# A state-space scan made in one pass from masked decay matrices, among the projections, in place of seven halving rounds

## The reference, cut to what matters

```python
def ssd_scan(x, dt, a, bm, cm, d_skip, s0):      # Q = 128
    cum = jnp.cumsum(dtc * a.astype(F32), axis=2)
    xdt = xc * dtc[..., None]
    diff = cum[:, :, :, None] - cum[:, :, None, :]
    seg = masked_decay(diff, causal)               # one number per (i, j, head)
    scores = jnp.einsum('bcihn,bcjhn->bcijh', cc, bc) * seg
    y_intra = jnp.einsum('bcijh,bcjhp->bcihp', scores, xdt)
    # chunk states, carried over the chunks, then y_inter, then + x * d_skip
```

## Time and profile before

| | us |
|---|---|
| three runs | 3509.2, 3509.12, 3503.52 (median 3509.12) |
| the profiled execution, and its span | 3511.4, 3509.3 |
| TensorE busy, share of the span | 3158.2, 90% |
| VectorE, ScalarE, GpSimd busy | 1349.5, 970.1, 243.9 |
| mean granted TensorE clock, share of full speed | 0.934 |

### The profile page before, as it was taken

How to read it: one execution, slowest core, us unless ns; L and a number is a source line. 1 busy time by engine, 2 the same in 40 slices (tenths; PEclk the granted TensorE clock), 3 DMA queues, 4 the chain that set the end, 5 groups by cost and what they waited for, 6 DMA issues and landing times. The chain is left out here.

```text
span 3509.3 us, 48131 instructions
## 1 busy us (share of the span) xinstructions
PE 3158.2 (90%) x20921; PEld 2703.4 (77%) x20921; DVE 1349.5 (38%) x1691; ACT 970.1 (28%) x1326; POOL 243.9 (7%) x136
## 2 busy tenths in 40 slices
PE   6999997778889979999979999986898898899996
PEld 5999994456546669999969999844555474899996
DVE  3233234562734252322352323355436342523235
ACT  3222213232334242222152222231232350422222
POOL 0000000240600000000000000003224000000000
PEclk8999998789979989999989999997899899899998
DMA  8223261231010022232622233504110100223221
GB/s 272 72 66 84 67 215 25 96 109 34 8 52 3 12 64 77 65 89 61 210 60 65 75 83 111 171 0 144 61 41 1 54 1 22 74 61 90 72 62 47
DMA packets 367123, 261.22 MB, mean 74 GB/s; under 512 B 39372, under 2 KB 318200, under 8 KB 366840
## 3 DMA queue, kind: packets, MB, share of 16 engines
q1 hardware_dynamic: 366968, 258.94, 24.5%
HBM read 255.34 MB, written 3.57 MB: 74 GB/s over the span
## 5 line engine op out<-in xcount | busy, mean ns | idle before, releaser
L679 PE MATMUL banks<-h_hi,w_split 128*128 128x320 f32 x5376 | 1184.3, 309 | 0.5 <-DVE mod L1476 0.5
L679 PEld LDWEIGHTS banks<-h_hi,w_split 128*128 128x128 f32 x5376 | 899.0, 188 | 0.7 <-issue 0.7
L679 PE MATMUL banks<-h_lo,w_split 128*128 128x320 f32 x2688 | 830.6, 309 | 0.0
L679 PE MATMUL banks<-hid_hi,w_split 128*128 128x320 f32 x2816 | 624.5, 310 | 0.0
L1530 DVE TENSOR_TENSOR w_split<-w_slots,w_split 128x2048 fp32r<-128x2048 f32 x152 | 348.1, 2292 | 453.3 <-ACT w_split L1119 453.0
L679 PEld LDWEIGHTS banks<-h_lo,w_split 128*128 128x128 f32 x2688 | 504.5, 188 | 0.0
L1119 ACT ACTIVATE arena<-banks 128x640 f32<-128x640 f32 (+6 forms) x340 | 174.9, 546 | 1106.4 <-PE banks L679 763.2
L679 PEld LDWEIGHTS banks<-hid_hi,w_split 128*128 128x128 f32 x2816 | 472.1, 188 | 1.2 <-issue 1.2
L679 PE MATMUL banks<-hid_lo,w_split 128*128 128x320 f32 x1408 | 435.0, 309 | 0.0
L1119 ACT ACTIVATE w_split<-w_slots 128x2048 fp32r<-128x2048 f32 x152 | 289.9, 1909 | 451.2 <-PE banks L679 442.8
L618 PE MATMUL banks<-h_mod,w_slots 128*128 128x512 f32 (+5 forms) x1344 | 380.0, 443 | 3.6 <-DVEq L1753 2.9
(11 more groups left out here) (220 smaller groups left out, 2682.4 us busy)
## 6 DMA issues: line engine op xcount, KB each, us to landing
w_slots<-in_ffn_w_gu SPq DMA_DIRECT2D x176, 512.0 KB, 5.1
w_slots<-in_ffn_w_down SPq DMA_DIRECT2D x64, 384.0 KB, 3.3
w_slots<-in_w_mod SPq DMA_DIRECT2D x12, 2048.0 KB, 8.0
w_slots<-in_ffn_w_down SPq DMA_DIRECT2D x64, 320.0 KB, 4.0
h_mod<-in_w_mod SPq DMA_DIRECT2D x9, 2048.0 KB, 8.0
mixed<-in_w_mod SPq DMA_DIRECT2D x9, 2048.0 KB, 9.9
arena<-in_w_mod SPq DMA_DIRECT2D x6, 2048.0 KB, 14.8
w_slots<-in_w_in SPq DMA_DIRECT2D x6, 2048.0 KB, 8.5
```

Source lines behind the costliest of these rows:

```text
L679: ins = mm(banks[:, b0 + hf, 0:HALF], w[:, k, :], x[:, k, t], start=w is wlo and k == 0, stop=w is whi and x is hi and k == kt - 1, skip_g ...
```

## The change

The ssd scan leaves the halving rounds. Its data is laid with tokens on partitions: PE turns the convolved x and B in chunks (`turn_xb`), z is projected straight into that layout (`first_rows`), and dt comes out of one job "sm", which also carries the last 64 rows of cq and the 32 of kr. For each chunk, `steps` on DVE makes two 128x512 products of a triangle and dt a; PE multiplies these by another triangle (`past`) and adds both directions into one bank; ACT takes the exponential (`decays`): all decay ratios of the chunk for four heads. PE makes C by B for the two groups (with B zeroed in one half of the partitions, by POOL); DVE masks it and multiplies it with the decays, once for each direction (`scores`), and PE multiplies by x dt (`values_ssd`). Chunk states and carried states are 16 and 16 small products; POOL makes x times skip and the two weighted x.

All that is written between the projections, which now include everything the hgrn scan needs (f0 to f3, hq, iv, g). Its jobs use four banks (`p_cols`), in two 320-column halves. B and C are projected once, not with each group doubled: 15 jobs and iv stand ahead of the one remaining scan, counting z as two. The levels of that scan carry cq0, ckv, qd0, qd1, kd at levels 0, 1, 3, 5, 7, and the six mod pieces at levels 1 to 6, behind the side job of the same level. The six mod weights share slot 1, one after another; the slots are no longer taken in turn. The parameter loads fall from 43 to 24 per layer.

```diff
+SLOT_FILLS = (("zx", "fi", "a", "d", "o0"), ("bcs", "qf", "g") + tuple(f"mod{i}" for i in range(MOD_LATE, MOD_FILLS)) + ("o1",))
+FILL_DMAS = dict(bcs=4, a=2, d=5)
...
-    jobs = ["x0", "x1", "dt", "b0", "b1", "c0", "c1", "z0", "sel0", "sel1", "z1", "sel2", "sel3", "y0", "ms0"]
...
+                fill("bcs", [(w[:, :, 0:256], w_in[:, :, C_BC:C_BC + 256]), (w[:, :, 256:320], w_in[:, :, P:Q_RANK]),
+                             (w[:, :, 320:352], w_in[:, :, C_KR:C_KR + ROPE]), (w[:, :, 352:360], w_in[:, :, C_DT:C_DT + 8])])
                 fill("qf", [(w_slot("qf", 8, 512), w_in[:, :, C_CQH:C_CQH + 512])])
...
+                fill("g", [(w_slot("g", 8, 256), w_in[:, :, C_G:C_G + 256])])
+                w = w_slot("a", 8, 256)
+                fill("a", [(w[:, :, 0:P], w_in[:, :, 0:P]), (w[:, :, P:256], w_in[:, :, C_CKV:C_CKV + P])])
+                fill("mod12", [(w_slot("mod12", 8, 512), w_mod_of(l, 12))])
+                fill("mod13", [(w_slot("mod13", 8, 512), w_mod_of(l, 13))])
                 pieces = []
...
+                for i in range(14, MOD_FILLS):
+                    fill(f"mod{i}", [(w_slot(f"mod{i}", 8, 512), w_mod_of(l, i))])
+
+                fill("o1", [(w_slot("o1", 8, 512), w_out[:, :, 512:1024])])
...
-                            ins.then_inc(s["done"], 1)
-                run("dt", W_DT, 0, 8, H, 8)
-                weights("bc")
-                w2 = w_slot("bc", 8, 512)
-                for g, name in enumerate(("b0", "b1", "c0", "c1")):
-                    run(name, w2, g * P, P, H, 8)
-                def spread(d):
-
-                    j = job[f"sel{d}"]
...
+                    pe.wait_ge(s["rb_ready"], o["rb_ready"] + 2 * c + 2)
+                    if c >= 2:
+                        pe.wait_ge(s["e_done"], o["e_done"] + c - 1)
+                        pe.wait_ge(s["y_added"], o["y_added"] + c - 1)
+                    else:
+                        pe.wait_ge(s["ex_ready"], o["ex_ready"] + 1)
+                        pe.wait_ge(s["s0_copied"], o["s0_copied"] + 1)
+                        pe.wait_ge(s["xb_copied"], o["xb_copied"] + NCH)
+                    for d in range(2):
+                        ins = mm(banks[:, 4 + c % 2, :], past[:, d], STEP[:, c % 2, d], start=d == 0, stop=d == 1)
+                    ins.then_inc(s["d_done"], 1)
+                    cols = slice(c * P, (c + 1) * P)
...
+                    for g in range(2):
+                        ins = mm(banks[:, 6 + c % 2, g * P:(g + 1) * P], BZ[g][:, cols], CC[:, cols], start=True, stop=True)
+                    ins.then_inc(s["cb_done"], 1)
+
+                def values_ssd(c):
+
+                    pe.wait_ge(s["vd_ready"], o["vd_ready"] + 1)
+                    pe.wait_ge(s["sc_ready"], o["sc_ready"] + 2 * c + 2)
+                    for h in range(4):
+                        for d in range(2):
+                            ins = mm(banks[:, 6 + c % 2, 256 + h * 64:320 + h * 64], SCORE[:, c % 2, d, h * P:(h + 1) * P],
+                                     XDT[:, d, c, h * 64:(h + 1) * 64], start=d == 0, stop=d == 1)
+                    ins.then_inc(s["pv_ssd"], 1)
...
+                    for t in range(4):
+                        for d in range(2):
+                            c = 4 if t == 3 else (t, 3 - t)[d]
+                            for g in range(2):
+                                ins = mm(banks[64 * g:64 * g + 64, 4 + t // 2, (2 * (t % 2) + d) * P:(2 * (t % 2) + d + 1) * P],
...
+                            rows = slice(64 * g, 64 * g + 64)
+                            ins = mm(banks[:, 4 + 2 * (c % 2) + g, d * P:(d + 1) * P], CC[rows, c * P:(c + 1) * P],
+                                     STATE[rows, c, d], start=True, stop=True)
...
+                turn_xb()
+                first_rows("za", w_zx, 0, (0, 1, 2, 3))
+                turn_dt()
...
+                first("f0", w_qf, 2 * P, P)
+                decay_sums()
+                first("f1", w_qf, 3 * P, P)
+                score_ssd(0)
+                score_ssd(1)
+                weights("fi")
+                first("f2", w_fi, 0, P)
+                values_ssd(0)
+                values_ssd(1)
+                score_ssd(2)
+                score_ssd(3)
+                first("f3", w_fi, P, P)
+                values_ssd(2)
+                values_ssd(3)
+                score_ssd(4)
+                first("hq0", w_qf, 0, P)
+                values_ssd(4)
...
+                chunk_states()
+                first_rows("iva", w_fi, 256, (0, 1, 2, 3))
+                carried(0)
+                carried(1)
+                first_rows("ivb", w_fi, 256, (4,))
+                first_used("ivb", 0)
+                carried(2)
+                carried(3)
+                turn_state()
+                weights("g")
+                first("g0", w_g, 0, P)
...
+                side_at = {0: ("cq0", "a", 0), 1: ("ckv", "a", P), 3: ("qd0", "d", 0), 5: ("qd1", "d", P), 7: ("kd", "d", 2 * P)}
...
+                                     q[rows, h // 2, cols], start=True, stop=True)
+                        ins.then_inc(s["att_done"], 1)
+                    if lev in side_at:
+                        name, fill, c0 = side_at[lev]
+                        if lev in (0, 3):
+                            weights(fill)
+                        if lev >= 2:
+                            pe.wait_ge(mod_done, mod_at[l, MOD_LATE + min(lev - 2, MOD_FILLS - MOD_LATE - 1)] + 1)
+                        side(name, w_slot(fill, 8, 256 if fill == "a" else 512), c0, P)
+                        if lev == 1:
+                            side_used(name)
+                    if 1 <= lev <= MOD_FILLS - MOD_LATE:
+                        i = MOD_LATE + lev - 1
+                        weights(f"mod{i}")
+                        pe.wait_ge(s["side_freed"], o["side_freed"] + len([x for x in side_at if x <= lev]))
+                        mod_rows(l, i, 6)
+                        pe.wait_ge(mod_row, mod_at[l, i] + 1)
+                        pe.sem_inc(w_used[1], 1)
...
+                def decays(c):
+                    act.wait_ge(s["d_done"], o["d_done"] + c + 1)
+                    f(STEP[:, c % 2, 0], banks[:, 4 + c % 2, :], ACT.Exp).then_inc(s["e_done"], 1)
+
+                forget(0)
+                act.wait_ge(s["cum_done"], o["cum_done"] + 1)
+                f(DECAYS, banks[:, 4, 0:120], ACT.Exp).then_inc(s["ex_ready"], 1)
+                forget(1)
+                decays(0)
+                decays(1)
+                forget(2)
+                decays(2)
+                decays(3)
+                forget(3)
+                decays(4)
...
+
+                    return v.tensor_tensor(dst.rearrange("p c (h n) -> p (c h) n", h=4), src.rearrange("p c (h n) -> p (c h) n", h=4),
+                                           bc(w.rearrange("p c h -> p (c h)").unsqueeze(2), [P, 20, 64]), ALU.mult)
+
+                def steps(c):
...
-                                src_c, dst_c = (t, t + 1) if d < 2 else (3 - t, 2 - t)
-                                link(v.scalar_tensor_tensor(out=SIN[rows, dst_c, d, rows], in0=SIN[rows, src_c, d, rows],
-                                                            scalar=DEC[rows, d // 2, d % 2, src_c:src_c + 1], in1=cs[rows, d, rows],
...
+                def scores(c):
+                    dve.wait_ge(s["cb_done"], o["cb_done"] + c + 1)
+                    dve.wait_ge(s["d_done"], o["d_done"] + c + 1)
+                    masked = STEP[:, c % 2, 1].rearrange("p (d g n) -> p d g n", d=2, g=2)
+                    finish(v.tensor_tensor(masked, bc(banks[:, 6 + c % 2, 0:256].rearrange("p (g n) -> p g n", g=2).unsqueeze(1), [P, 2, 2, P]),
+                                           bc(upto.unsqueeze(2), [P, 2, 2, P]), ALU.mult), "cbm_done", c + 1)
+                    dve.wait_ge(s["e_done"], o["e_done"] + c + 1)
+                    if c >= 2:
+                        dve.wait_ge(s["pv_ssd"], o["pv_ssd"] + c - 1)
+                    decay = STEP[:, c % 2, 0].rearrange("p (g h n) -> p g h n", g=2, h=2)
+                    for d in range(2):
+                        v.tensor_tensor(SCORE[:, c % 2, d].rearrange("p (g h n) -> p g h n", g=2, h=2), decay,
+                                        bc(masked[:, d].unsqueeze(2), [P, 2, 2, P]), ALU.mult).then_inc(s["sc_ready"], 1)
+
+                def add_values(c):
+                    dve.wait_ge(s["pv_ssd"], o["pv_ssd"] + c + 1)
+                    dve.wait_ge(s["xs_ready"], o["xs_ready"] + 1)
+                    finish(v.tensor_tensor(YS[:, c], YS[:, c], banks[:, 6 + c % 2, 256:512], ALU.add), "y_added", c + 1)
...
+                dve.wait_ge(s["xb_copied"], o["xb_copied"] + NCH)
+                steps(0)
+                steps(1)
+                for d in range(2):
+                    ins = weighted(XDT[:, d], XTOK, DT[:, d])
+                finish(ins, "vd_ready", 1)
+                dve.wait_ge(s["ex_ready"], o["ex_ready"] + 1)
```

(44 more changed lines are left out.)

953 lines of the change are left out of this document (475 added, 478 removed).

## The result

The changed kernel took **3271.5 us** (median of four executions, 3267.3 to 3273.2), against 3508.8 for the kernel before beside it (3503.5 to 3509.2). The ratio is 0.9327, with a 95% interval of 0.9315 to 0.9339: 237 us less. Executions over 1.5% above the fastest of their kernel are left out of the ratios. I had forecast 3323 with a range of 3292 to 3372. The sign and the kind of gain were right; the size was 51 us too small, and the result lies outside the range.

What follows compares the result with a forecast made beforehand. The ssd scan was taken to cost time because PE had nothing else written beside it. Per layer 310.6 + 85.0 - 197 - 105.7 = 92.9, in both 186, giving 3323 us, range 3292 to 3372.

Steps and rivals of the forecast that it cites:

- Stage A: First projection to level 0 of the hgrn scan (before: the second scan), per layer: 310.6 us before, 197 forecast.
- The near end of the price for repeating operands: DVE products whose operands repeat along the row cost 0.69 us per 512 columns; the far end was 1.7.
- Rival 2: VectorE and GpSimd hold PE in stage A, 8 to 25 us per layer, 3340 to 3373 us; chance 0.15.
- stage A, the scan's PE work: Decay, C-by-B, value, state and carry products, transposes and small sums on PE: together 33 us per layer.
- stage A, four waits and the clock: PE waits at the turning, carries with `turn_state`, and behind `turn_y`: 8 us; clock loss 6; per layer.
- stage B, levels 2, 4, 6: Levels of the remaining scan carrying a mod piece alone: 12.9 us each, 38.6 per layer.
- stage B, levels 0, 1, 3, 5 and the late load: Level 0 with cq0 15.2 us, levels with side job plus mod piece 16.1 each, late weights 3.5 at level 3.
- what follows level 7, and the rest: Everything behind level 7 and outside both stages: same work in the same order, no change, 0 us.
- two such thin places: The turning and the carry in stage A, where PE's clock would dip: 6 us added per layer.
- number 1: Rival: PE never waits, no clock loss, loads in time; at most 35 us less, down to 3290; chance 0.12.
- The turning: Turning x and B in stage A through two buffers that ACT empties by two copies per chunk: 3.5 us of waits.
- rival 3: Late mod weights in stage B at 14.8 us a load: 20 us more per layer, 3363 us; chance 0.09.

Runs made afterwards that it cites:

- g1_one_tile: Changed kernel with projection g1 multiplying one of its eight weight tiles, 7.6 us of PE work less a layer; 3261.8 us.
- steps_twice: Changed kernel with each of the ten DVE products of `steps` made twice, 6.5 us more of DVE a layer; 3275.8 us.
- before_levels_warm: Kernel before with eight idle products behind each mod piece at levels 0 to 5 of the first scan; 3483.4 us.
- the two runs with the filled wait: Nine idle products in PE's 4.84 us wait for the norm of ckv: in the kernel before 3491.0 us, in the changed kernel 3263.5.
- vd_later_4: Changed kernel with four idle products (1.9 us) in front of the product vd; two executions, 3268.0 and 3356.0 us.
- norms_warm: Changed kernel with idle products ahead of the cache turn and in the layer norms' waits, all ahead of the wait they fill; median 3273.7 us.
- kept_warm: Changed kernel with idle products for all of PE's waits of 3 us and more, 25 of them placed behind their wait; 3310.5 us.

## Why the prediction was wrong in size

**What held.** Stage A is TensorE's own work laid end to end (g1_one_tile: 7.5 for 7.6). The near end of the price for repeating operands was right:

```profile
L1842 DVE TENSOR_TENSOR arena<-arena 128x512 f32<-128x512 f32 x10 | 6.5, 688 | 0.7 <-ACT arena L1222 0.6
L1828 DVE TENSOR_TENSOR arena<-cst,arena 128x512 f32<-128x512 f32 x10 | 6.3, 684 | 0.0
```

0.68 to 0.69 us for 512 elements, as in the earlier trace rows. The decay products (0.87), C by B and values (0.22), the wait of `turn_state` (2.27 against 2.5) and the one behind `turn_y` (1.92 against 2.2) came as worked out. Rival 2 didn't come: GpSimd's products took 2.33 us instead of the 4 that I had scaled from its strided sums, and it held DVE once, for 2 us:

```profile
642.79 2.41 DVE L1869 COPY arena<-arena 64x20 f32<-64x20 f32 x2
```

```profile
642.84 2.33 POOL L2078 TENSOR_TENSOR mixed<-arena 128x1280 f32<-128x1280 f32 x1 [28.69 <-DVE arena L1866]
```

Two equal copies; by the view of that line one took 168 ns and the other, beside GpSimd, 2227. The Trainium skill, SBUF — State Buffer, "Who interferes with whom", says that a copy in its two-port form and a GpSimd instruction shut each other out for the whole instruction. These two lines agree with it. It cost PE nothing: steps_twice hid 6.5 us more of DVE. That slack I had put at about 1 us ahead of `score_ssd(2)`, which was too little, though I charged nothing for it in the sum.

**What failed, term by term** (layer 0; the sum of the misses is 52 over both layers):

| step of the prediction | forecast | measured | miss, both layers |
|---|---|---|---|
| stage A, projections | 150.3 | 152.0 | -3 |
| stage A, the scan's PE work | 33 | 28.5 | 9 |
| stage A, four waits and the clock (measured: PE's idle time) | 14 | 6.4 | 15 |
| stage B, levels 2, 4, 6 | 38.6 | 34.8 | 8 |
| stage B, levels 0, 1, 3, 5 and the late load | 67.1 | 62.4 | 9 |
| what follows level 7, and the rest | 0 | -14 in all | 14 |

*The clock* is the largest part, some 30 of the 52 us by this account, and it failed at three steps. "Stage A has two such thin places, the turning and the carry: I add 6": the stage holds 0.98, and behind the carry g0 and g1 take 18.57 us instead of 17.4, 1.2 lost where I had 6 (in the table it stands with the projections). "12.9 each" for the mod levels came from a level of the first scan, where scores took 4.80 instead of 2.9; I had both rows and named the difference, and then carried over the slow one. before_levels_warm shows that levels 3 to 5 take 10.8 to 11.1 at the full clock; the new ones took 11.9, 11.2 and 11.7. And "what follows level 7 is the same work in the same order" is true of the work, not of its time: the two runs with the filled wait show 12.4 us of clock in it, a term that I had put at nothing. By my own reading the clock had one rival for a gain, number 1 with 35 us; the result is 18 us beyond even that, because it counted only the three terms that I had charged and none of the stretches left alone.

*The scan's PE work.* The step "a 128-column product takes 1.95 / 8 = 0.24", used for 16 state and 16 carry products, 7.7 us. They took 1.9 and 2.2 (the rows of lines 899 and 913 above): 0.12 to 0.14 each. The nearest row was another one: 20 score products of 64 rows in 2.9 us, 0.145 each. All of these use half of the array, 64 rows or 64 columns, and by these figures two of them take together what one of the full products of the earlier trace rows takes, 0.24.

*The turning.* I added 3.5 of waits to 1.8 of transposes. It took 3.0 in all, since ACT's copies overlap the next chunk's transposes.

*The mod piece behind a side job.* I took 3.3 us for it, from a level of the first scan. It took 2.6 (776.68 to 779.28), at levels 1, 3 and 5.

*Late weights.* "I charge 3.5 at level 3", and rival 3 with 20 a layer. The waits came (4.62, 1.93, 4.37, 4.58), and without the loads stage B was 0.9 us shorter. The price of a wait isn't its length; it is what it adds to the chain beside it.

## What to carry to other kernels

Before a duration is carried to a new place, its clock has to be known: take it from a row at the full clock, and add the clock's loss as a term of its own, in stretches that the change leaves alone too. When a serial scan on small products becomes one pass, its place between projections may be the smaller part: here it brought 12 of 124 us a layer. A pair of half-array products took what one full product took, 0.24 us.

## What the runs showed of the hardware that I had not expected

For how long TensorE's clock stays at its lower level (1.2 of 2.4 GHz) isn't told by the wait ahead of it or by the work behind it. Behind one and the same 4.84 us wait, with the same work after it, it was 31, 15, 10, 9, 31 and 17 us in these runs. It went with the instant of the fall: 2.0 to 2.8 us before the end of the wait in the long cases, 0.6 to 1.3 in the short ones, without exception in 20. These are single profiled executions, and what sets the instant stays open.

In attention the clock fell to 0.50 with TensorE busy for 93.23 of 96 us, and each of the three stretches of 96 us (two in vd_later_4, one in norms_warm) cost some 40 us; kept_warm had shorter ones, 38 and 55 us. By the times it happens in some executions of a kernel and not in others. The Trainium skill, TensorE: Matmul & The Clock Gate, Part 1, has activity release the throttle; in these stretches a busy engine went without for up to 96 us. What starts such a stretch stays open. Both are likely part of the reason why keeping TensorE warm gave 21 and 13 us in the kernel before, 8 in the changed kernel, and a loss when all waits were filled.
